# A two-block network on one core: modulation sums and relus in PSUM, logits in head pairs, five modulation chunks in later stages

## What is computed

```python
mod = silu(c) @ w_ada + b_ada          # 6 vectors of 1024: sh1, sc1, ga1, sh2, sc2, ga2
proj = (rmsnorm(x, g_attn) * (1 + sc1) + sh1) @ w_in       # qa, ka, va, qb, ckv, qi, ki, wi
logits = einsum('bqhd,bkd->bqhk', qi, ki)                  # 8 indexer heads of 64
score = einsum('bqh,bqhk->bqk', wi, relu(logits))          # then the 128 best keys of each query
x = x + ga1 * (mixed @ w_out)
h2 = rmsnorm(x, g_ffn) * (1 + sc2) + sh2
x = x + ga2 * ((silu(h2 @ gate) * (h2 @ up)) @ w_down)
mod_2 = silu(c_2) @ mod_w_2 + mod_b_2  # shift, scale, gate of block two: 3 vectors of 1024
```

## Time and profile before

| | us |
|---|---|
| three runs | 1198.83, 1200.85, 1205.87 |
| median | 1200.85 |
| the profiled execution's own time | 1196.73 |
| its span, first to last instruction | 1194.9 |

### The profile page before, as it was taken

One profiled execution on the slowest core, in us unless ns is written; L12 is line 12 of the kernel. 1 busy time (PEld: TensorE's weight loads), 2 busy tenths in 40 slices (PEclk: granted clock), 3 DMA queues, 4 the chain that ended last, 5 costly groups with the idle time before them and its releaser, 6 DMA issues.

```text
span 1194.9 us, 14091 instructions
## 1 busy us (share of the span) xinstructions
PE 1095.4 (92%) x5110; PEld 865.0 (72%) x5110; DVE 761.5 (64%) x1344; ACT 420.2 (35%) x596; POOL 446.3 (37%) x155
## 2 busy tenths in 40 slices
PE   2988899689997999999999999799999999698997
PEld 2666679346676788888887888677887777576885
DVE  3499799658865664464463011369999998985323
ACT  4223322656732412222213222232215777241222
POOL 0034135414414143444343444404353655623340
PEclk9888999889999999999998999989999999899998
DMA  9967223104013145435432222303423232312311
GB/s 314 345 205 233 73 72 101 41 1 142 1 36 114 62 141 175 140 111 170 140 119 84 94 91 92 103 16 106 140 71 106 71 101 76 105 36 71 105 36 70
DMA packets 127724, 128.85 MB, mean 108 GB/s; under 512 B 3699, under 2 KB 125883, under 8 KB 127675
## 3 DMA queue, kind: packets, MB, share of 16 engines
q1 hardware_dynamic: 127040, 127.98, 32.9%
q10 hardware_dynamic: 635, 0.23, 0.1%
HBM read 126.10 MB, written 2.10 MB: 107 GB/s over the span
## 4 chain that ended last, share of the span: by engine, by line
PE 37%; issue 35%; DVE 12%; POOL 11%; ACT 3%; ACTq 1%; POOLq 0%; DMA 0%; DVEq 0%; SPq 0%
POOL w_lo L541 10%; PE bank L633 8%; PE bank L634 8%; PE bank L635 8%; DVE bank L1887 3%; DVE ada_acc L1511 3%; PE bank L858 2%; PE bank L869 1%; PE bank L894 1%; PE bank L708 1%; POOL lru_lo L611 1%; PE bank L773 1%; ACT w_hi L1125 1%; DVE ada_acc L1508 1%; PE bank L884 1%
## 5 line engine op out<-in xcount | busy, mean ns | idle before, releaser
L541 POOL TENSOR_TENSOR w_lo<-w_stage,w_hi 128x2048 fp32r<-128x2048 f32 x79 | 371.5, 4702 | 631.1 <-ACT w_hi L1125 631.1
L633 PE MATMUL bank<-act_hi,w_hi 128*128 128x512 f32 x856 | 341.7, 399 | 7.7 <-POOL w_lo L541 7.7
L634 PE MATMUL bank<-act_lo,w_hi 128*128 128x512 f32 x856 | 335.3, 392 | 0.0
L635 PE MATMUL bank<-act_hi,w_lo 128*128 128x512 f32 x856 | 335.0, 391 | 0.0
L1125 ACT ACTIVATE w_hi<-w_stage 128x2048 fp32r<-128x2048 f32 x81 | 154.8, 1912 | 261.7 <-PE bank L635 261.6
L633 PEld LDWEIGHTS bank<-act_hi,w_hi 128*128 128x128 f32 x856 | 162.3, 190 | 45.9 <-issue 7.4
L634 PEld LDWEIGHTS bank<-act_lo,w_hi 128*128 128x128 f32 x856 | 162.4, 190 | 34.5 <-issue 1.9
L635 PEld LDWEIGHTS bank<-act_hi,w_lo 128*128 128x128 f32 x856 | 162.1, 189 | 34.4
L1887 DVE SCALAR_TENSOR_TENSOR bank<-v_pad,vcol,bank 128x512 f32<-128x512 f32 x232 | 153.9, 751 | 0.0
L1816 DVE TENSOR_TENSOR tmp<-bank,tmp 128x512 f32<-128x512 f32 x22 | 15.2, 692 | 115.7 <-PE bank L635 112.4
L1778 DVE SCALAR_TENSOR_TENSOR xT<-bank,mod,xT 128x512 f32<-128x512 f32 x16 | 12.0, 749 | 109.9 <-PE bank L635 109.9
(11 more groups left out here) (272 smaller groups left out, 1651.7 us busy)
## 6 DMA issues: line engine op xcount, KB each, us to landing
w_stage<-in_w_in SPq DMA_DIRECT2D x30, 1024.0 KB, 5.1
ada_stage<-in_w_ada SPq DMA_DIRECT2D x24, 1024.0 KB, 10.7
w_stage<-in_w_gu SPq DMA_DIRECT2D x22, 1024.0 KB, 5.0
w_stage<-in_w_out SPq DMA_DIRECT2D x12, 1024.0 KB, 5.1
ada_stage<-in_mod_w SPq DMA_DIRECT2D x12, 1024.0 KB, 5.3
w_stage<-in_w_down SPq DMA_DIRECT2D x8, 1024.0 KB, 5.2
w_stage<-in_pw_w SPq DMA_DIRECT2D x4, 1024.0 KB, 5.1
w_stage<-in_w_down SPq DMA_DIRECT2D x4, 768.0 KB, 4.6
```

Of the source, the lines that this page charges most:

```text
L541: nc.gpsimd.tensor_tensor(w_lo[b][:], w_stage[b][:], w_hi[b][:].bitcast(F32), ALU.subtract).then_inc(s_lo, 1)
L633: pe.matmul(dst, wh, rhs_hi(k), start=(first and k == 0), stop=False)
L634: pe.matmul(dst, wh, rhs_lo(k), start=False, stop=False)
L635: mm = pe.matmul(dst, wl, rhs_hi(k), start=False, stop=(last and k == n_k - 1))
```

## The change

1. **Sums in PSUM.** `ada_step` keeps its two partial sums in bank 6 and writes only the last two into `ada_acc`. The addition of the halves (line 1498) is gone; PE's `ada_products` does four matmuls of one column in place of two. The gate/up loop sums in bank 4.
2. **Relus in PSUM, logits in pairs.** A step computes two heads into two banks (4 and 5, or 2 and 3), one ACTIVATE takes both relus in place, and DVE reads PSUM. The first pair comes in the middle of tile 6, the next behind it, and so on to tile 11. A pair waits for the sums of the pair before last. Tiles from 6 on alternate between banks 0 and 1. The turn of the indexer weights (`wiT`) comes behind tile 5, the second turn of `ckv` behind tile 13 and not 11. DVE does two slices of a chunk behind each head's sum.
3. **Chunks moved.** Chunks 16 to 20 leave the projection. 16 to 19 take the place of 21 to 24 in the `w_out` stage, and the `fold` that needs them goes there. 24 to 34 are the loop's. 20 to 23 and 35 (`ADA_LATE`) are new between the loop and `w_down`: SP loads 35 during the last pass of the loop and the other four into `act_hi` and `act_lo` when the last gate/up tile is done, ahead of chunk `C_DOWN + 2`. DVE adds them up ahead of `lam_t`, PE multiplies behind the first two tiles.
4. The loop over `w_down` is written out. SP loads `w_in` chunks 2 and 3 earlier.

```diff
--- before.py
+++ after.py
-ADA_FIRST = 8
-ADA_WINDOW = {0: 3, 1: 3, 2: 3, 3: 0, 4: 2, 5: 2}
-ADA_AFTER = {2: 0, 3: 1, 4: 2, 5: 1, 6: 2, 7: 1, 8: 2, 9: 1, 10: 1, 11: 1, 12: 1}
-ADA_ATT = ADA_FIRST + sum(ADA_WINDOW.values())
-ADA_LOOP = ADA_ATT + 4
+ADA_FIRST, ADA_ATT, ADA_OUT, ADA_LOOP, ADA_DOWN = 8, 16, 20, 24, 35
+ADA_EARLY = 3
+ADA_AFTER = {5: 1, 6: 2, 8: 1, 9: 1, 10: 1, 11: 1, 12: 1}
...
+ADA_LATE = [ADA_DOWN] + list(range(ADA_OUT, ADA_LOOP))
...
-PAIRS = [(i, h) for i in range(1, TT) for h in range(NH)]
-PAIRS_PER_TILE = 4
...
+PAIRS = [(i, g) for i in range(1, TT) for g in range(NH // 2)]
...
+ADA_STEPS = 2
+def in_bank(t):
+    return t if t < 6 else t % 2
+def logit_banks(p):
+    return (2, 3) if p % 2 else (4, 5)
...
+            w_in_dma(2)
+            w_in_dma(3)
...
+                if ADA_FIRST + 4 + n < ADA_ATT:
+                    ada_dma(ADA_FIRST + 4 + n)
...
+            for n in range(12):
+                k0, kn = ((0, 8), (8, 8), (16, 6))[n % 3]
+                w_dma(C_DOWN + n, w_cols(a["w_down"], k0, kn, n // 3 * NCOL))
+                if n == 0:
+                    sp.wait_ge(s_adaacc, ADA_ORD[ADA_LATE[0]])
+                    late_dma(0)
+                if n == 1:
+                    sp.wait_ge(s_wused, C_DOWN)
+                    for b in range(1, len(ADA_LATE)):
+                        late_dma(b)
...
+                    if halfway and k == n_k // 2:
+                        halfway()
...
+            def ada_products(c):
                 o = ADA_ORD[c]
                 pe.wait_ge(s_adaacc, o + 1)
                 for m in range(2):
...
+                    for s in range(2):
+                        mm = pe.matmul(bank[7][:, 2 * c + m:2 * c + m + 1],
+                                       ada_acc[ADA_ACC[o]][:, s, m * P:(m + 1) * P], ones[:, 0:1], start=(s == 0), stop=(s == 1))
+                mm.then_inc(s_adamm, 1)
+            def late_products(b):
+                c = ADA_LATE[b]
+                pe.wait_ge(s_adaacc, ADA_ORD[c] + 1)
+                for m in range(2):
+                    q = 2 * (c - ADA_OUT) + m
+                    for s in range(2):
+                        mm = pe.matmul(bank[5][:, q:q + 1], late_acc(b)[:, s, m * P:(m + 1) * P], ones[:, 0:1],
...
+                t = t_acc[0]
+                if t in (6, 7):
+                    pe.wait_ge(s_free, t - 5)
+                elif t >= 8:
+                    pe.wait_ge(s_free, t - 1 + (t - 2 >= 5))
                 t_acc[0] += 1
-                return b
+                return bank[in_bank(t)]
             pairs = list(enumerate(PAIRS))
             def logits():
...
+                if not pairs:
+                    return
+                p, (i, g) = pairs.pop(0)
+                if p == 0:
+                    pe.wait_ge(s_free, 7)
+                elif p == 1:
+                    pe.wait_ge(s_ckvn, 1)
+                    pe.wait_ge(s_wi, 1)
+                else:
+                    pe.wait_ge(s_score, 2 * (p - 1))
+                n = P * (i + 1)
+                for m in range(2):
+                    half = slice(HD * m, HD * m + HD)
+                    mm = pe.matmul(bank[logit_banks(p)[m]][:, 0:n], qiT[half, g, i * P:(i + 1) * P], kiT[half, 0:n],
+                                   start=True, stop=True)
+                mm.then_inc(s_lg, 1)
...
-                        tile(acc_bank()[:], b, slice(m * P, (m + 1) * P), KD, hi, lo).then_inc((s_acc, s_wused)[m], 1)
+                        tile(acc_bank()[:], b, slice(m * P, (m + 1) * P), KD, hi, lo,
+                             halfway=logits if n >= 3 else None).then_inc((s_acc, s_wused)[m], 1)
...
-                        if (n, m) == (3, 0):
+                        if (n, m) == (2, 1):
...
-                        if (n, m) == (5, 1):
+                        if (n, m) == (6, 1):
                             pe.wait_ge(s_ckv, CKV_STEPS)
+                            pe.wait_ge(s_score, 2 * len(PAIRS) - 2)
                             for t in range(TT):
-                                mm = pe.transpose(bank[6][:, t * P:(t + 1) * P], ckv[:, t, :], ident[:])
+                                mm = pe.transpose(bank[4][:, t * P:(t + 1) * P], ckv[:, t, :], ident[:])
...
+                if m2 == 0:
+                    for b in range(len(ADA_LATE)):
+                        late_products(b)
...
+                if not pairs:
+                    return
+                p, (i, g) = pairs.pop(0)
+                b, n = logit_banks(p)[0], P * (i + 1)
+                act.wait_ge(s_lg, p + 1)
+                nc.scalar.activation(psum[:, b:b + 2, 0:n], psum[:, b:b + 2, 0:n], ACT.Relu).then_inc(s_relu, 1)
...
+                    act.wait_ge(s_wiT, 1)
+                    nc.scalar.activation(wi_sb[:].rearrange("p t h -> p (t h)"), bank[3][:, 0:TT * 8], ACT.Copy).then_inc(s_wi, 1)
...
+                late = ADA_LATE.index(c) if c in ADA_LATE else None
+                acc = late_acc(late) if late is not None else ada_acc[ADA_ACC[o]]
                 if t == 0:
-                    ada_wait(dve, c)
+                    if late is None:
+                        ada_wait(dve, c)
+                    else:
+                        dve.wait_ge(s_late_ada[late], 16)
+                    dve.wait_ge(s_adaacc, o)
+                src, w = (ada_stage[c] if late is None else late_stage[late])[:, t, :], c_act[:, 0 if c < ADA1 else 1, t:t + 1]
+                part = bank[6][:, (t % 2) * NCOL:(t % 2 + 1) * NCOL]
+                if t == KD - 2 and late is None:
                     last = [q for q in range(o) if ADA_ACC[q] == ADA_ACC[o]]
                     if last:
                         dve.wait_ge(s_adamm, last[-1] + 1)
-                src, w = ada_stage[c][:, t, :], c_act[:, 0 if c < ADA1 else 1, t:t + 1]
-                dst = acc[:, t % 2, :]
                 if t < 2:
-                    i = V.tensor_scalar(dst, src, w, None, ALU.mult)
+                    i = V.tensor_scalar(part, src, w, None, ALU.mult)
                 else:
                     dve.wait_ge(s_adastep, steps[0] - 1)
-                    i = V.scalar_tensor_tensor(dst, src, w, dst, ALU.mult, ALU.add)
-                i.then_inc(s_adastep, 1)
-                steps[0] += 1
...
+                    i = V.scalar_tensor_tensor(part if t < KD - 2 else acc[:, t % 2, :], src, w, part, ALU.mult, ALU.add)
+                i.then_inc(s_adaacc if t == KD - 1 else s_adastep, 1)
+                steps[0] += t < KD - 1
...
+            def score_sum(p, m):
+                i, g = PAIRS[p]
+                h, n, s = 2 * g + m, P * (i + 1), 2 * p + m
+                src, w = bank[logit_banks(p)[m]][:, 0:n], wi_sb[:, i, h:h + 1]
+                dve.wait_ge(s_relu, p + 1)
+                if h == 0:
+                    V.tensor_scalar(score[i][:], src, w, None, ALU.mult).then_inc(s_score, 1)
+                else:
+                    dve.wait_ge(s_score, s)
+                    V.scalar_tensor_tensor(score[i][:], src, w, score[i][:], ALU.mult, ALU.add).then_inc(s_score, 1)
+            window = list(range(ADA_FIRST, ADA_ATT))
+            ada_more(ADA_EARLY * ADA_ITEMS, window)
...
+            dve.wait_ge(s_wi, 1)
+            for p in range(len(PAIRS)):
+                for m in range(2):
+                    score_sum(p, m)
+                    ada_more(ADA_STEPS, window)
...
-            fold("g_ffn", SC2, 1)
...
+            ada_done[0] = 0
+            residual(C_OUT, lambda k: modc(GA1 + k), turn=2, between=ADA_TILE, chunks=list(range(ADA_ATT, ADA_OUT)))
+            dve.wait_ge(s_adamm, ADA_DVE)
+            ms = slice(2 * ADA_ATT, 2 * ADA_OUT)
+            V.tensor_tensor(mod[:, ms], bank[7][:, ms], vcol[:, ms], ALU.add).then_inc(s_mod, 1)
+            dve.wait_ge(s_mod, 4)
+            fold("g_ffn", SC2, 1)
...
+                        V.tensor_scalar(bank[4][:, 0:NCOL], src, w, None, ALU.mult).then_inc(s_adastep, 1)
                     else:
                         dve.wait_ge(s_adastep, j * (KD - 1) + (ada_steps + t))
...
+                        V.scalar_tensor_tensor(ada2_acc[:] if t == KD - 1 else bank[4][:, 0:NCOL], src, w, bank[4][:, 0:NCOL],
+                                               ALU.mult, ALU.add).then_inc(s_adaacc if t == KD - 1 else s_adastep, 1)
...
+            steps[0] += KF // 2 * (KD - 1)
+            dve.wait_ge(s_fflo, 2 + KF)
+            ada_done[0] = 0
+            ada_more(ADA_ITEMS * len(ADA_LATE), ADA_LATE)
...
+            dve.wait_ge(s_adamm, len(ADA_ORD))
+            for m0, m1 in ((2 * ADA_OUT, 2 * ADA_LOOP), (2 * ADA_DOWN, 72)):
+                V.tensor_tensor(mod[:, m0:m1], bank[5][:, m0 - 2 * ADA_OUT:m1 - 2 * ADA_OUT], vcol[:, m0:m1], ALU.add).then_inc(s_mod, 1)
+            dve.wait_ge(s_mod, 10)
+            V.tensor_scalar(scale1[:, 3, :], mod[:, GA3:GA3 + KD], 1.0, None, ALU.add).then_inc(s_mod, 1)
```

245 lines of the change are left out of this document (79 added, 166 removed).

## The result

| | before | changed kernel |
|---|---|---|
| median of 20 runs, us | 1198.4 | 1202.75 |
| lowest, highest | 1191.76, 1206.12 | 1199.25, 1214.38 |
| profiled execution's span | 1194.9 | 1203.2 |
| ratio of the times | | 1.0049, 95% interval 1.0026 to 1.0072 |

The ratio makes it +5.9 us on 1198.4 (3.1 to 8.6). The forecast was +2.8, so the measured change lies in its range of -2 to +6, at the upper edge. The forecast time of 1203.7 came within 1 us of the measured 1202.75, and that is luck: it was added to a median of three runs, 1200.85, which is 2.5 above the median of twenty, and this made up for most of the 3.1 by which the change was forecast too small. The signs of its terms hold. The loss at the turn is larger than forecast, and some of what the profile shows differs as much between executions of one kernel.

The account below looks back on a forecast made before the run. PE, busy 92% of the span, was taken as the bound. Projection -10.8, `w_out` +1.6 and turn +12.0 make +2.8 us: 1199.5 on the profiled 1196.73, 1203.7 on the median 1200.85. Range -2 to +6, or 1194.5 to 1210.

Parts of the forecast that it names:

- the turn: From gate/up to `w_down`: +12.0 us, from a wait on `w_lo`, a lower clock and the five late chunks' products.
- The projection: Input projection, tiles 4 to 17: PE's surplus over 5.46 us a tile falls from 36.6 to 25.8, -10.8 us.
- the "best" of the working: Projection's logit pairs: 0.70, 0.92 and 1.13 us, 11.0 in all, where the forecast took 13.8.
- The keys are found by 194.4, 4.4 us ahead of PE: End of the projection: DVE's sums end at 143.6, its best keys at 194.4, PE at 198.8.
- what matters: Projection: POOL does not stop DVE's eight operations a chunk, which cost what nine did; bank sums averaged 751 ns.
- The rival that a bank costs DVE more: Late chain of 40 operations: 0.09 us more each, +3.6, change +6.4 or +9.1, time 1207 to 1210; chance 0.2.
- by the trace the rule adds nothing: Projection's logits: visits double from 6 to 12, but the rows show no drain beyond lengths already used; no price.
- wait for `w_lo`: Start of `w_down`: `w_lo` of chunk `C_DOWN + 2` ready at 672.7, PE wants it at 667.5, +5.2 us.
- clock: Start of `w_down`, behind PE's wait: 14 matmuls at granted clock 0.50 take 5.94 us for 3.2, +2.7.
- products: `w_down`, behind tile 1: PE's products of the five late chunks, 5 x 0.82, +4.1 us.
- The 0.82 a chunk: PE's cost of one chunk's products, read in the projection and used there and for the late chunks: 0.82 us.
- Late transfers hidden by this same wait: Start of `w_down`: SP's late loads from 640.2 land by 660, within PE's wait, adding no cost.

Follow-up runs that it names:

- pairs at the ends: Changed kernel with both logit pairs of a tile behind its end, none halfway: median 1206.05 us, ratio 1.0052 to the kernel before.
- both profiles: Profiles of the changed kernel (median 1202.75 us) and of the same kernel run again unedited in another set (1203.46 us, ratio 1.0055).
- the logarithm first: Changed kernel with DVE's first two steps of the logarithm's chain ahead of the five late chunks: median 1195.44 us, ratio 0.9980 to the kernel before.

## Why the prediction was right and wrong

**The projection.** Forecast -10.8, measured -12.0 and -10.5: right, and mostly by its own terms. From tile 4's start to tile 14's (74.60 to 153.95) are 79.35 us, where ten tiles of 5.46 are 54.6: a surplus of 24.8 for 25.8 forecast. The pairs took 0.70, 0.92 and 1.13, the "best" of the working, 2.8 us less in all than the 13.8 that it took; that gain is partly lost on the halves of the tiles, 0.3 each, which the working did not have.

**DVE behind it.** "The keys are found by 194.4, 4.4 us ahead of PE" failed. The sums ended on time (144.4 less the 1.2 by which tile 4 starts later, for 143.6), but the causal minimum reads two SBUF tensors like the steps that the working counted as stopped by POOL, and it met a `w_lo`. The slack was nil. That it cost nothing here is luck, since DVE and PE ended in a tie; it cost 1.2 us as soon as PE got faster.

**That the sums' PSUM bank is "what matters".** For the score sums the views agree (384 columns: 1189 ns to 613). For the modulation sums the step failed. Put back into SBUF in the new order they are blocked again and the projection is as long. So the gain in PE's time comes from the rest: the logits in pairs, the relus in place, fewer chunks and their order. These were not tried one by one, and their shares are not shown. The rival that a bank costs DVE more fell for its main steps: 0.87 a pair in both, and the late chain of 40 took 16.7 us where the forecast had 16.4. By the fixed parts that the Trainium skill gives in VectorE: DVE Perf Modes, section on the TRN2 errata, each would have been 0.065 us longer, an estimate, and the trace does not agree. The first step of a chain did get longer (0.87 for 0.60 a pair); it reads SBUF and writes the bank, for which those fixed parts are not given.

**The price of a visit.** The Trainium skill, TensorEngine Tiling, section Tiling Modes, has a change of mode drain TensorE; the prediction gave it no price and took it that "by the trace the rule adds nothing". That failed. Six visits of logits less (pairs at the ends) saved 2.7 us, 0.45 a visit. So the trace agrees that a visit costs, and the gain forecast for the projection had no term for the six that were added. Whether a drain or the tile's interrupted pace makes the cost is not told apart.

**`w_out`.** +1.6 forecast, +1.8 measured in both profiles.

**The turn.** Forecast +12.0, measured +15.0 and +13.7. The mechanism was right step by step, and the logarithm first took 8 us away. The sizes, by the first profile:

| term | forecast | measured |
|---|---|---|
| wait for `w_lo` | +5.2 | +6.7 |
| clock | +2.7 | +1.8 behind the wait (36 matmuls in 9.98 for 8.2), +2.5 behind the products (5.68 for 3.2), -1.1 in the first tiles |
| products | +4.1 | +4.9 |

The wait was longer since PE came 1.1 us earlier: its 96 matmuls took 23.73, with 8 at the low clock and not 14 as in the earlier trace rows. DVE's part (16.7 from the end of `fold` to the second step, for 16.4) gave 0.3. The mis-sized term is the products. The 0.82 a chunk was read where their start hides under the end of a tile; 40 in a row take 0.12 each with nothing to hide under, 0.99 a chunk. And the clock fell behind them (+2.5), a cost that the working had only behind waits and left out here. "Late transfers hidden by this same wait" was right, and they were the next in line once it was gone.

**The rest.** The ratio gives +5.9 and the bold terms +4.8 to +5.0, so 1 us is open; the start and the end, which were shortest in the profile before, may hold it. Start, attention, gate/up's first tiles and the last stages move by 2 to 7 us between executions of kernels that do not differ there. The attention took 124.8 to 132.1 in thirteen profiles, two of them shown above (126.18 and 132.09). The working treated one profile's clock as the kernel's. And two errors have opposite signs: the projection gained 1.2 more than forecast in the first profile (0.3 less in the second), and the turn lost 3.0 more (1.7 in the second).
